# The first layer norm of an encoder layer, computed by tokens in place of features

## The chip, the cores and the metric

One core of a Trainium2 chip runs the whole kernel. The metric is the device time of one execution in microseconds (us), lower being better. The engines named below are TensorE (PE, with its weight loads PEld), VectorE (DVE), ScalarE (ACT), GpSimd (POOL) and SyncE (SP, which issues transfers).

## The reference

One encoder layer: 16 meta tokens are put ahead of 512 tokens of width 1024, and four layer norms stand around a feed-forward block, a token mixer and a second feed-forward block. The change touches the first norm, whose result `h` feeds the first feed-forward block and the residual.

```python
def layer_norm(x, g, b):
    xf = x.astype(jnp.float32)
    mu = jnp.mean(xf, axis=-1, keepdims=True)
    xc = xf - mu
    var = jnp.mean(xc * xc, axis=-1, keepdims=True)
    return (xc * lax.rsqrt(var + LN_EPS) * g + b).astype(x.dtype)

def swiglu(h, w_gate, w_up, w_down):
    return (jax.nn.silu(h @ w_gate) * (h @ w_up)) @ w_down
...
    h = layer_norm(jnp.concatenate([meta, x], axis=1), ln_in_g, ln_in_b)
    for i in range(DEPTH):
        h = layer_norm(DN_ALPHA * h + 0.5 * swiglu(h, ffn1_w_gate[i], ffn1_w_up[i], ffn1_w_down[i]),
                       ffn1_ln_g[i], ffn1_ln_b[i])
```

## The kernel before, in words

Activations lie with features on the partitions: `X` and `H` are 128 x 8 x 528 float32 (eight tile columns `k` of 128 features, 528 tokens), and `xs` holds the norm's scaled output as two float16 parts, high (`xs[:, 0]`) and low (`xs[:, 1]`). Matmuls of float32 quality are made of three float16 products (high x high, low x high, high x low). So each weight chunk, too, is split. A chunk is the gate and up weights of one tile of 128 hidden features, 128 x 2048 float32 in one of two slots of `stage`. VectorE takes its absolute maximum (`chunk_max`), GpSimd the maximum over partitions, VectorE makes a power-of-two scale of it (`chunk_scale`), ScalarE writes the high part to `wsp` (`split_hi`) and VectorE the low part (`chunk_lo`, which signals `w_ready`). SyncE loads the next chunk into a slot once its low part is written.

The order on each engine is written out by hand, and engines meet at semaphores. The first norm (L = 0) ran like the others, in two halves of 264 tokens: VectorE sums the eight tiles (`x_sum`, L1770), TensorE multiplies by a matrix of 1/1024 to spread the mean over the partitions (L465), VectorE subtracts it (`centre`, L1257), ScalarE squares (L918), TensorE adds the squares up over features (L470), ScalarE takes the root (L932), VectorE the reciprocal (L1277) and multiplies (L1281), and ScalarE writes the high part of `xs` (L943) and `H` (L945) with gain and bias as scale and bias columns. VectorE writes the low part (`split_lo`, L1271). `layer_norm_scales` (L1745 on) computes the powers of two for three norms from the parameters. Between these steps stand the maxima, scales and splits of chunks 0 and 1.

The first feed-forward block starts with `gu_tile` for tile 0 (`first=True`): for each tile column `k` it waits for the high part (`x_hi`) and the low part (`x_ready`), 12 matmuls of 264 columns each. Tiles 1 to 21 need the whole of `xs` and their own chunk, 96 matmuls each. ScalarE applies Silu to a tile's gate half (L958), VectorE multiplies by the up half (`hidden_tile`, L1342). Then VectorE turns to the chunk two tiles on.

## Time and profile before

| what | value |
|---|---|
| median of 3 runs | 1099.26 us (1098.03 to 1104.86) |
| the profiled execution's own time | 1098.44 us |
| its span | 1096.6 us |
| TensorE busy | 1005.5 us (92%) |
| VectorE busy | 730.0 us (67%) |
| ScalarE busy | 385.6 us (35%) |
| mean granted clock of TensorE | 0.972 of 2.4 GHz |

The span is the time from the first to the last instruction of one profiled execution, and its own time contains it. A busy TensorE is not TensorE at its peak, since matmuls are pipelined. The shares are means over stages with different limits: what an edit at the start is worth is read from the start.

### The profile page before, as it was taken

The page shows a single profiled execution, that of the slowest core. Times are in us where ns is not written, and L with a number is a line of the kernel's source. Part 1 is how long each engine was busy: PE and PEld are TensorE (multiplying, and loading weights), DVE is VectorE, ACT ScalarE, POOL GpSimd, SP SyncE. Part 2 cuts the span into 40 slices and gives each one's busy share as a digit, 9 for nine tenths or more (in the row PEclk, how much of TensorE's full clock was granted, in tenths as well). Part 3 has the DMA queues.
Part 4 walks back from the last instruction along what each step waited for, and adds up shares of the span by engine and source line. Part 5 has one row for each costly group of instructions (what it writes and reads, how often), then busy time and mean ns, then how long its engine had stood idle before and what let it go on. Part 6 is the DMA issues. An engine that isn't in the chain of part 4 may idle for free.

```text
span 1096.6 us, 16402 instructions
## 1 busy us (share of the span) xinstructions
PE 1005.5 (92%) x6604; PEld 658.2 (60%) x6604; DVE 730.0 (67%) x1188; ACT 385.6 (35%) x492; POOL 33.8 (3%) x96
## 2 busy tenths in 40 slices
PE   2799999999899997999996889779999999989995
PEld 1588888888688874895565434434444444434443
DVE  7756666668865657777658857676666666876645
ACT  2722222224511117655234742362222222541105
POOL 1000000000000000000000000000000000000000
PEclk9899999999899998999998989889999999999998
DMA  4232232323313220221211002213232232312202
GB/s 157 71 114 101 90 111 80 115 77 140 109 54 106 96 77 1 78 78 40 76 40 39 1 1 77 77 39 113 79 115 103 88 115 90 145 56 103 105 1 78
DMA packets 25168, 88.70 MB, mean 81 GB/s; under 512 B 2859, under 2 KB 5123, under 8 KB 25123
## 3 DMA queue, kind: packets, MB, share of 16 engines
q1 hardware_dynamic: 24256, 87.24, 22.7%
q10 hardware_dynamic: 867, 0.85, 0.3%
q8 instruction: 29, 0.48, 0.2%
q14 instruction: 16, 0.13, 0.0%
HBM read 85.99 MB, written 2.10 MB: 80 GB/s over the span
## 4 chain that ended last, share of the span: by engine, by line
PE 75%; DVE 15%; ACT 7%; issue 2%; DMA 1%; ACTq 0%; POOL 0%; DVEq 0%
PE PS L485 35%; PE PS L521 20%; PE PS L576 8%; PE PS L872 3%; DVE cmax L1308 3%; DVE wsp L1330 3%; PE PS L470 2%; ACT wsp L951 2%; ACT H L945 2%; DVE X L1257 1%; PE PS L560 1%; PE PS L850 1%; DVE big L1408 1%; ACT xs L943 1%; PE PS L698 1%
## 5 line engine op out<-in xcount | busy, mean ns | idle before, releaser
L485 PE MATMUL PS<-xs,wsp 128*128 128x264 f16 (+1 forms) x3168 | 471.6, 312 | 12.8 <-ACT xs L943 8.1
L485 PEld LDWEIGHTS PS<-xs,wsp 128*128 128x128 f16 x3168 | 310.6, 98 | 173.8 <-issue 13.5
L951 ACT ACTIVATE wsp<-stage,wscale 128x2048 f16<-128x2048 f32 (+2 forms) x73 | 156.5, 2144 | 370.5 <-DVE wscale L1294 198.6
L1330 DVE SCALAR_TENSOR_TENSOR wsp<-stage,wscale,wsp 128x2048 f16<-128x2048 f32 (+2 forms) x73 | 184.6, 2529 | 113.9 <-ACT wsp L951 113.9
L521 PE MATMUL PS<-big,wsp 128*128 128x264 f16 (+1 forms) x1584 | 238.5, 314 | 11.6 <-DVE big L1408 9.5
L521 PEld LDWEIGHTS PS<-big,wsp 128*128 128x128 f16 x1584 | 155.8, 99 | 94.0 <-DVE big L1408 12.8
L1308 DVE TENSOR_REDUCE cmax<-stage 128x1 f32<-128x2048 f32 (+2 forms) x73 | 179.7, 2461 | 3.9
L1342 DVE SCALAR_TENSOR_TENSOR big<-PS,oscale,tmp_a 128x528 f32 (+3 forms) x44 | 33.4, 758 | 75.8 <-ACT tmp_a L958 75.8
L958 ACT ACTIVATE tmp_a<-PS,oscale 128x528 f32<-128x528 f32 (+1 forms) x44 | 30.5, 693 | 135.9 <-PE PS L485 135.9
L576 PE MATMUL PS<-xs,wsp 128*128 128x264 f16 (+1 forms) x384 | 67.0, 328 | 0.1
L1842 POOL PARTITION_ALL_REDUCE call<-cmax x73 | 29.5, 404 | 984.2 <-DVE cmax L1308 984.2
L470 PE MATMUL PS<-tmp_b,ones 128*128 128x264 f32 (+1 forms) x128 | 36.2, 445 | 17.5 <-ACT tmp_b L918 17.5
L576 PEld LDWEIGHTS PS<-xs,wsp 128*128 128x128 f16 x384 | 35.8, 98 | 24.4 <-issue 1.9
L872 PE MATMUL PS<-xs,wsp 128*128 128x512 f16 x192 | 42.4, 379 | 3.2 <-DVE X L1354 2.1
L470 PEld LDWEIGHTS PS<-tmp_b,ones 128*128 128x128 f32 x128 | 27.9, 223 | 26.1 <-ACT tmp_b L918 21.1
L918 ACT ACTIVATE tmp_b<-X 128x264 f32<-128x264 f32 (+1 forms) x64 | 23.9, 416 | 49.5 <-DVE X L1257 45.7
L576 PE MATMUL PS<-wsp,xs 128*88 128x256 f16 (+2 forms) x408 | 39.5, 257 | 1.7 <-ACT kT L1013 1.7
L981 ACT ACTIVATE big<-big,hscale 128x528 f16<-128x528 f32 (+1 forms) x44 | 30.3, 722 | 29.1 <-DVE big L1408 26.5
L576 PEld LDWEIGHTS PS<-wsp,xs 128*88 128x88 f16 (+2 forms) x408 | 38.0, 113 | 3.5 <-ACT kT L1013 2.5
L1408 DVE SCALAR_TENSOR_TENSOR big<-big,hscale 128x528 f16<-128x528 f32 (+1 forms) x44 | 31.6, 755 | 5.0 <-ACT big L981 3.8
L872 PEld LDWEIGHTS PS<-xs,wsp 128*128 128x128 f16 x192 | 18.5, 98 | 26.8 <-DVE wsp L1330 2.6
L1366 DVE SCALAR_TENSOR_TENSOR X<-PS,oscale,H 128x528 f32<-128x528 f32 (+1 forms) x16 | 12.2, 760 | 27.5 <-PE PS L521 27.4
(178 smaller groups left out, 694.4 us busy)
## 6 DMA issues: line engine op xcount, KB each, us to landing
stage<-in_gate SPq DMA_DIRECT2D x44, 512.0 KB, 3.7
stage<-in_up SPq DMA_DIRECT2D x44, 512.0 KB, 4.5
stage<-in_down SPq DMA_DIRECT2D x32, 704.0 KB, 4.9
stage<-in_w_in SPq DMA_DIRECT2D x16, 512.0 KB, 4.6
stage<-in_w_out SPq DMA_DIRECT2D x8, 512.0 KB, 4.3
X<-in_xT SPq DMA_DIRECT2D x2, 1056.0 KB, 6.9
out_T<-H SPq DMA_DIRECT2D x8, 256.0 KB, 2.0
stage<-in_w_in SPq DMA_DIRECT2D x2, 576.0 KB, 4.3
```

The lines of the kernel that those rows point to most:

```text
L470: nc.tensor.matmul(PS[:, ln_bank(L, 1, h), 0:ln_width(L)], ones[:, :], squares[:, n % 4, 0:ln_width(L)], start=k == 0, stop=k == KD - 1).t ...
L485: return nc.tensor.matmul(dst, w, x, start=k == 0 and wp + xp == 0, stop=k == KD - 1 and xp == 1)
L521: mm = nc.tensor.matmul(dst, w(wp, k), x, start=k in (0, split_at) and wp + xp == 0, stop=k + 1 in (kt, split_at) and xp == 1)
L576: mm = nc.tensor.matmul(dst, x if lhs_is_x else w, w if lhs_is_x else x, start=k == 0 and wp + xp == 0, stop=k == KD - 1 and xp == 1)
L872: mm = nc.tensor.matmul(acc(1, 2 * (n % 2)), w, tokens(1, xs[:, xp, k, :]), start=gla and k == REP and wp + xp == 0, stop=not gla and k == ...
L951: nc.scalar.activation(wsp[:, slot, 0, 0:cols], stage[:, slot, 0:cols], ACT.Copy, scale=wscale[:, slot:slot + 1]).then_inc(w_hi, 1)
L958: nc.scalar.activation(tokens(f, tmp_a[:, s, :]), acc(f, 4 * s), ACT.Silu, scale=oscale[:, slot:slot + 1]).then_inc(silu_ready, 1)
L981: nc.scalar.activation(hid_s[:, m, 0, ln_cols(2 * f)], hid[:, m + 2, ln_cols(2 * f)], ACT.Copy, scale=hscale[:, i:i + 1]).then_inc(hs_hi, 1)
L1308: nc.vector.tensor_reduce(cmax[:, one], stage[:, slot, 0:cols], AX.X, ALU.max, apply_absolute_value=True).then_inc(w_max, 1)
L1330: nc.vector.scalar_tensor_tensor(wsp[:, slot, 1, 0:cols], stage[:, slot, 0:cols], wscale[:, one], wsp[:, slot, 0, 0:cols], ALU.mult, ALU.s ...
L1342: nc.vector.scalar_tensor_tensor(tokens(f, hid[:, m + 2, :]), acc(f, 4 * s + 2), oscale[:, slot:slot + 1], tokens(f, tmp_a[:, s, :]), ALU. ...
L1408: nc.vector.scalar_tensor_tensor(hid_s[:, m, 1, t], hid[:, m + 2, t], hscale[:, i:i + 1], hid_s[:, m, 0, t], ALU.mult, ALU.subtract).then_ ...
```

## The change

The input comes with tokens on the partitions: four tiles `x_tok` of 128 tokens x 1024 features, in the memory of `X`, loaded by four transfers with chunk 0 after the second and chunk 1 last. Mean and variance are now one number per partition, held in `tok_stat`: a sum along the free axis on VectorE (on ScalarE for tile 2), a square with an accumulated sum on ScalarE with minus the mean as bias, a root and a reciprocal of one column, and one `tensor_scalar` that adds minus the mean and multiplies (`tok_norm`). TensorE transposes each 128 x 128 block into PSUM banks 4 to 7 (`turn`): tile columns 0 to 3 of all token tiles ahead of the first products, 4 to 7 inside tile 0 (`turn_late`). Gain and bias are applied where PSUM is read: ScalarE writes all high parts and the even tile columns of `H`, VectorE the odd ones (`tok_affine`) and the low parts (`tok_lo`). The 16 meta tokens come as a 128 x 128 tile, 8 partitions to a token, with a 128 x 128 matrix that averages over each 8; they have a path of their own beside the token tiles. The other norms are as they were; their counts of semaphores start at L = 1. The identity, until now loaded behind the first norm, is loaded at the start. The diff without the meta tokens' path, the semaphores' declarations and renumberings:

```diff
-        x_loaded = [sem(f"x_loaded{i}") for i in range(2)]
+        x_tok = X[:, :, :].rearrange("p k t -> p (k t)")[:, 0:N_TOK * D_MODEL].rearrange("p (i d) -> p i d", i=N_TOK)
+        meta_x, meta_ones = tmp_a[:, 0, 0:P], tmp_a[:, 0, P:2 * P]
+        tok_scratch = big[:, 0:(N_TOK + 2) * D_MODEL].rearrange("p (i d) -> p i d", d=D_MODEL)
...
-            for h in range(2):
-                sp.dma_start(X[:, :, token_half(0, h)], xT[h].rearrange("p (k t) -> p k t", k=KD)).then_inc(x_loaded[h], 16)
+            for i in range(N_TOK):
+                sp.dma_start(x_tok[:, i, :], x_in[i]).then_inc(x_loaded[i], 16)
+                if i == 1:
+                    load_gu(0, 0, 0)
+            load_gu(0, 1, 1)
...
-                    if L:
-                        pe.wait_ge(*((res_half, L) if h == 0 else (res_done, 2 + KD * L)))
-                        last = X[:, KD - 1, token_half(L, h)]
-                    else:
-                        pe.wait_ge(x_summed, h + 1)
-                        last = x_sum[:, token_half(L, h)]
-                    nc.tensor.matmul(PS[:, ln_bank(L, 0, h), 0:ln_width(L)], ones[:, :], last, start=L == 0, stop=True).then_inc(mean_ready, 1)
...
+            def turn(k, i):
+
+                return nc.tensor.transpose(PS[:, 4 + k % 4, P * i:P * (i + 1)], x_tok[:, i, P * k:P * (k + 1)], ident[:, :])
...
+                pe.wait_ge(ident_loaded, 16)
+                for i in range(N_TOK):
+                    pe.wait_ge(tok_normed, i + 1)
+                    for k in range(4):
+                        mm = turn(k, i)
+                        if i == N_TOK - 1:
+                            mm.then_inc(tok_turned, 1)
+                    if i == 1:
+                        pe.wait_ge(meta_normed, 1)
+                        nc.tensor.transpose(PS[:, 3, 0:P], meta_x, ident[:, :]).then_inc(meta_turned, 1)
+
+            def turn_late(k):
+
+                pe.wait_ge(x_ready, k - 3)
+                for i in range(N_TOK):
+                    mm = turn(k, i)
+                mm.then_inc(tok_turned, 1)
...
+                    if f == 0:
+                        pe.wait_ge(meta_lo, 1)
                     for k, g in itertools.product(range(KD), range(2)):
+                        if f == 0 and g == 1 and k >= 1 and k + 3 < KD:
+                            turn_late(k + 3)
...
-            layer_norm(0)
+            start_tokens()
...
+            act.dma_start(tmp_a[:, 0, 0:2 * P], meta_in).then_inc(meta_loaded, 16)
+            act.dma_start(ident[:, :], ident_in).then_inc(ident_loaded, 16)
...
+            def tok_square(i):
+                act.wait_ge(tok_mean, i + 1)
+                nc.scalar.activation(tok_scratch[:, i, :], x_tok[:, i, :], ACT.Square, bias=tok(MEAN, i),
+                                     accum_out=tok(VAR, i)).then_inc(tok_sq, 1)
+
+            def tok_root(i):
+                act.wait_ge(tok_sq, i + 1)
+                nc.scalar.activation(tok(ROOT, i), tok(VAR, i), ACT.Sqrt, bias=eps[:, 0:1],
+                                     scale=1.0 / D_MODEL).then_inc(tok_std, 1)
...
+                tok_square(0)
+                tok_root(0)
...
+                tok_square(1)
+                tok_root(1)
+                act.wait_ge(x_loaded[2], 16)
+                nc.scalar.activation(tok_scratch[:, N_TOK + 1, :], x_tok[:, 2, :], ACT.Copy, accum_out=tok(SUM, 2)).then_inc(tok_sum_2, 1)
+                tok_square(2)
+                tok_root(2)
+                split_hi(0, 0, GU_COLS)
+                tok_square(3)
+                tok_root(3)
...
+                for k in range(KD):
+                    if k == 5:
+                        split_hi(GU[0] + 1, 1, GU_COLS)
+                    x = PS[:, 4 + k % 4, 0:SEQ]
+                    act.wait_ge(tok_turned, k + 1)
+                    nc.scalar.activation(xs[:, 0, k, N_META:T], x, ACT.Identity, scale=par_s[:, C_G[0] + k:C_G[0] + k + 1],
+                                         bias=par_s[:, C_B[0] + k:C_B[0] + k + 1]).then_inc(x_hi, 1)
+                    if k % 2 == 0:
+                        nc.scalar.activation(H[:, k, N_META:T], x, ACT.Identity, scale=par[:, C_G[0] + k:C_G[0] + k + 1],
+                                             bias=par[:, C_B[0] + k:C_B[0] + k + 1]).then_inc(h_in, 1)
+
...
+            def tok_total(i):
+                dve.wait_ge(x_loaded[i], 16)
+                nc.vector.tensor_reduce(tok(SUM, i), x_tok[:, i, :], AX.X, ALU.add).then_inc(tok_sum, 1)
...
+            def tok_minus_mean(i, signal, at):
+                dve.wait_ge(signal, at)
+                nc.vector.tensor_scalar(tok(MEAN, i), tok(SUM, i), -1.0 / D_MODEL, None, ALU.mult).then_inc(tok_mean, 1)
+
+            def tok_norm(i):
+                dve.wait_ge(tok_std, i + 1)
+                nc.vector.reciprocal(tok(ROOT, i), tok(ROOT, i)).then_inc(tok_rstd, 1)
+                dve.wait_ge(tok_rstd, i + 1)
+                nc.vector.tensor_scalar(x_tok[:, i, :], x_tok[:, i, :], tok(MEAN, i), tok(ROOT, i),
+                                        ALU.add, ALU.mult).then_inc(tok_normed, 1)
...
+            def tok_affine(k):
+                if k % 2:
+                    dve.wait_ge(x_hi, k + 1)
+                    nc.vector.tensor_scalar(H[:, k, N_META:T], PS[:, 4 + k % 4, 0:SEQ], par[:, C_G[0] + k:C_G[0] + k + 1],
+                                            par[:, C_B[0] + k:C_B[0] + k + 1], ALU.mult, ALU.add).then_inc(h_in_v, 1)
+
+            def tok_lo(k):
+                dve.wait_ge(x_hi, k + 1)
+                dve.wait_ge(h_in_v if k % 2 else h_in, k // 2 + 1)
+                nc.vector.scalar_tensor_tensor(xs[:, 1, k, N_META:T], H[:, k, N_META:T], xscale[:, 0:1], xs[:, 0, k, N_META:T],
+                                               ALU.mult, ALU.subtract).then_inc(x_ready, 1)
+
...
+            dve.wait_ge(meta_loaded, 16)
+            nc.vector.tensor_reduce(tok(SUM, META), meta_x, AX.X, ALU.add).then_inc(meta_sum, 1)
+            tok_total(0)
+            tok_minus_mean(0, tok_sum, 1)
+            dve.wait_ge(meta_avg, 1)
+            nc.vector.tensor_scalar(tok(MEAN, META), PS[:, 3, P:P + 1], -1.0, None, ALU.mult).then_inc(meta_mean, 1)
+            tok_total(1)
+            tok_minus_mean(1, tok_sum, 2)
+            tok_norm(0)
+            meta_norm()
+            tok_norm(1)
             chunk_max(0, 0, 0, GU_COLS)
-            centre(0, 1)
+            tok_minus_mean(2, tok_sum_2, 1)
+            tok_total(3)
+            tok_minus_mean(3, tok_sum, 3)
             chunk_scale(0, 0, XF_GU[0])
...
+            meta_affine()
+            tok_norm(2)
             chunk_lo(0, 0, GU_COLS)
-            layer_norm(0, (1, 1, XF_GU[0]))
+            tok_norm(3)
+            dve.wait_ge(meta_hi, 1)
+            nc.vector.scalar_tensor_tensor(xs[:, 1, :, 0:N_META], H[:, :, 0:N_META], xscale[:, 0:1], xs[:, 0, :, 0:N_META],
+                                           ALU.mult, ALU.subtract).then_inc(meta_lo, 1)
+            for k in range(KD):
+                tok_affine(k)
+                tok_lo(k)
+                if k == 1:
+                    chunk_max(1, 1, 0, GU_COLS)
+                if k == 3:
+                    chunk_scale(1, 1, XF_GU[0])
...
-    tokens = np.concatenate([meta_tokens, x[0]], 0)
-    arrays = {"xT": kcols(tokens.T).reshape(P, KD, 2, HALF).transpose(2, 0, 1, 3).reshape(2, P, -1)}
+    segment = np.arange(P) // KD
+    block_mean = (segment[:, None] == segment[None, :]).astype(np.float32) / D_MODEL
+    arrays = {"x": x[0].reshape(N_TOK, P, D_MODEL), "meta": np.concatenate([meta_tokens.reshape(P, P), block_mean], 1)}
```

How the instructions stand now on two engines. In the rows a name is an instruction's output and inputs, and the bracket what it waits for.

The first place is VectorE in the norm. Before, from centring the first half on (`stats` is where sums and reciprocals lie, `cmax` a chunk's maximum, `call` the same over partitions):

```order
L1257 TENSOR_TENSOR X<-X,PS 128x264 [waits mean_ready,b_step]
L1257 TENSOR_TENSOR X<-X,PS 128x264 x7
L1308 TENSOR_REDUCE cmax<-stage 128x1 [waits w_loaded0]
...
L1308 TENSOR_REDUCE cmax<-stage 128x1 [waits w_loaded1]
L1330 SCALAR_TENSOR_TENSOR wsp<-stage,wscale,wsp 128x2048 [waits w_hi]
...
L1277 RECIPROCAL stats<-stats 128x264 [waits std_ready] x2
L1281 TENSOR_TENSOR X<-X,stats 128x528 [waits centred,rstd_ready]
L1281 TENSOR_TENSOR X<-X,stats 128x528 [waits centred] x2
L1271 SCALAR_TENSOR_TENSOR xs<-H,xscale,xs 128x528 [waits h_ready]
```

Behind the two halves' centring stand chunk 1's maximum, chunk 0's low part, the long reciprocals and the multiplications. After, from the second token tile's normalising to the fourth's:

```order
L1883 RECIPROCAL tok_stat<-tok_stat 128x1 [waits tok_std]
L1885 TENSOR_SCALAR X<-X,tok_stat 128x1024 [waits tok_rstd]
L1413 TENSOR_REDUCE cmax<-stage 128x1 [waits w_loaded0]
L1879 TENSOR_SCALAR tok_stat<-tok_stat 128x1 [waits tok_sum_2]
L1875 TENSOR_REDUCE tok_stat<-X 128x1 [waits x_loaded3]
L1879 TENSOR_SCALAR tok_stat<-tok_stat 128x1 [waits tok_sum]
...
L1885 TENSOR_SCALAR X<-X,tok_stat 128x1024 [waits tok_rstd]
L1435 SCALAR_TENSOR_TENSOR wsp<-stage,wscale,wsp 128x2048 [waits w_hi]
L1883 RECIPROCAL tok_stat<-tok_stat 128x1 [waits tok_std]
L1885 TENSOR_SCALAR X<-X,tok_stat 128x1024 [waits tok_rstd]
```

The centring passes over `PS` and the long reciprocals are gone, and chunk 1's maximum is no longer ahead of chunk 0's low part.

The second place is VectorE behind the first eviction, after (before, nothing but multiplications and low parts stood there):

```order
L1912 SCALAR_TENSOR_TENSOR xs<-H,xscale,xs 128x512 [waits h_in,x_hi]
L1906 TENSOR_SCALAR H<-PS,par 128x512 [waits x_hi]
L1912 SCALAR_TENSOR_TENSOR xs<-H,xscale,xs 128x512 [waits h_in_v,x_hi]
L1413 TENSOR_REDUCE cmax<-stage 128x1 [waits w_loaded1]
L1912 SCALAR_TENSOR_TENSOR xs<-H,xscale,xs 128x512 [waits h_in,x_hi]
L1906 TENSOR_SCALAR H<-PS,par 128x512 [waits x_hi]
L1912 SCALAR_TENSOR_TENSOR xs<-H,xscale,xs 128x512 [waits h_in_v,x_hi]
L1395 TENSOR_SCALAR cexp<-call 128x1 [waits w_all]
```

Chunk 1's maximum is now behind the low part of tile column 1 and ahead of that of column 2; the scale made from it follows after column 3.

The third place is ScalarE around chunk 1's split, where `xs` and `H` are written. Before, from tile column 3:

```order
L943 ACTIVATE xs<-X,par_s 128x528 [waits normed]
L945 ACTIVATE H<-X,par 128x528
L951 ACTIVATE wsp<-stage,wscale 128x2048 [waits w_scale]
L943 ACTIVATE xs<-X,par_s 128x528 [waits normed]
L945 ACTIVATE H<-X,par 128x528
```

The split stood ahead of tile column 4, two rows to a column. After, from `H` of column 2:

```order
L1033 ACTIVATE H<-PS,par 128x512
L1030 ACTIVATE xs<-PS,par_s 128x512 [waits tok_turned] x2
L1033 ACTIVATE H<-PS,par 128x512
L1059 ACTIVATE wsp<-stage,wscale 128x2048 [waits w_scale]
L1030 ACTIVATE xs<-PS,par_s 128x512 [waits tok_turned] x2
L1033 ACTIVATE H<-PS,par 128x512
```

It now stands ahead of column 5. Of eight rows on `H` four have gone to VectorE, and the source is `PS` in place of `X`.

On TensorE the column sums of ones are gone. Sixteen transposes, and one for the meta tokens, stand ahead of the products, and sixteen more inside tile 0 in groups of four, between the gate and the up products of tile columns 1 to 4, the group for column k waiting for the low part of column k - 4, whose bank it takes.

## Rows read from the trace of the kernel before

**Rows 1.** Chain of waits, first 75 us: start us, length us, what.

```profile
0.73 5.71 DMA X<-in_xT
...
6.46 7.30 DVE stats L1770 x2
...
15.87 2.81 DVE X L1257 x8
18.68 2.20 DVE cmax L1308
...
28.22 5.53 PE PS L470 x16
...
34.29 1.81 DVE stats L1277
...
38.41 0.72 ACT xs L943
...
42.72 1.89 ACT wsp L951
...
51.17 2.27 DVE wsp L1330
...
53.49 21.55 PE PS L485 x190
```

**Rows 2.** Windows: us; busy us (count) of PE, PEld, DVE, ACT, POOL; PEclk, DMA share, GB/s.

```profile
5.00:10.00 5.00, 0.00 (x0) 0.00 (x0) 3.54 (x1) 0.00 (x0) 0.00 (x0) 1.00 1.09 382
...
100.00:200.00 100.00, 100.00 (x892) 86.97 (x890) 61.59 (x88) 25.11 (x19) 3.50 (x10) 1.00 0.27 95
```

**Rows 3.** DMA issues of inputs: KB each, median us from issue to landing.

```profile
X<-in_xT SPq DMA_DIRECT2D x2, 1056.0 KB, 6.9
...
par<-in_params ACTq DMA_DIRECT2D x1, 38.5 KB, 1.9
```

**Rows 4.** VectorE in order of time, first of the scales: start us, us, what.

```profile
13.68 0.19 DVE L1747 TENSOR_REDUCE bmax<-par 128x6 f32<-128x48 f32 x1
```

**Rows 5.** VectorE groups by form: count, busy us, mean ns, idle before.

```profile
L1271 DVE SCALAR_TENSOR_TENSOR xs<-H,xscale,xs 128x512 f16<-128x512 f32 x8 | 6.0, 751 | 3.9 <-ACT H L945 3.7
...
L1292 DVE TENSOR_SCALAR cneg<-cexp 128x1 int32<-128x1 int32 x73 | 11.2, 154 | 2.5
...
L1298 DVE TENSOR_REDUCE hmax<-big 128x1 f32<-128x528 f32 x6 | 4.2, 693 | 0.0
...
L1478 DVE TENSOR_SCALAR tmp_b<-PS,par 128x528 f32<-128x528 f32 x4 | 3.1, 768 | 11.7 <-ACT tmp_a L1043 11.5
...
L1512 DVE TENSOR_SCALAR tmp_a<-tmp_a 128x528 f32<-128x528 f32 x4 | 1.7, 434 | 0.1
```

**Rows 6.** ScalarE groups by form.

```profile
L1177 ACT ACTIVATION_READ_ACCUMULATOR tmp_b<-tmp_b,smin 128x1 f32 x16 | 3.0, 186 | 0.0
...
L1200 ACT ACTIVATE xs<-PS,hscale 128x512 f16<-128x512 f32 x4 | 2.7, 676 | 4.6 <-PE PS L850 4.6
...
L1050 ACT ACTIVATE tmp_a<-tmp_a 128x1056 f32<-128x1056 f32 x2 | 2.2, 1084 | 0.0
...
L1013 ACT ACTIVATE kT<-PS,oscale 128x16 f32<-128x16 f32 x1 | 0.3, 263 | 0.0
```

**Rows 7.** TensorE, transposes by ident in the attention.

```profile
L832 PE MATMUL PS<-ident,tmp_b 128*128 128x128 f32 x56 | 9.0, 306 | 1.8 <-DVE tmp_b L1732 1.6
```

**Rows 8.** TensorE in order of time in tile 0, and windows of 1 us there.

```profile
39.27 7.07 PE L485 MATMUL PS<-xs,wsp 128*128 128x264 f16 x48 [0.82 <-DVE xs L1271]
...
41.00:42.00 1.00, 1.00 (x6) 0.72 (x5) 0.95 (x2) 1.00 (x3) 0.00 (x0) 0.50 0.00 0
...
43.00:44.00 1.00, 1.00 (x11) 0.87 (x10) 1.00 (x2) 1.00 (x1) 0.00 (x0) 1.00 0.00 0
```

**Rows 9.** VectorE in order of time, tile 0's hidden product and chunk 2.

```profile
53.34 0.76 DVE L1342 SCALAR_TENSOR_TENSOR big<-PS,oscale,tmp_a 128x528 f32<-128x528 f32 x1
...
59.55 2.35 DVE L1330 SCALAR_TENSOR_TENSOR wsp<-stage,wscale,wsp 128x2048 f16<-128x2048 f32 x1 [1.81 <-ACT wsp L951]
```

115 lines of the change are left out of this document (82 added, 33 removed).

## Prediction

> **What bounds the kernel now.** I read the chain of waits first, from the start of the span. Up to 53.49 us it runs through the first layer norm; from there TensorE's gate and up products follow one another [rows 1]. Its pieces are the first half of the input (5.71), the sums over the eight tiles (7.30), centring (2.81 twice), the first weight chunk's maximum (2.20), the squares' column sums (5.53), the reciprocal (1.81), a weight split on ScalarE (1.89) and the low half of chunk 1 on VectorE (2.27). Tile 1 of the gate and up products starts when that last one ends. The reader should take 53.49 as the number that decides. Behind it TensorE is busy for all of 100 us with 892 matmuls, one per 0.112 us, while VectorE is busy for 62 [rows 2]. A tile is 96 matmuls, 10.8 us. So what tile 1 gains in start, the end gains, as long as chunk 2 is ready in time and later stages, whose instructions are the same, don't care. The profiled execution's span is 1096.6 and its own time 1098.44; the median of the runs shown is 1099.26, 0.8 above. A change can be told from none here by about 1%, 11 us.
>
> **Inputs.** The input is now four token tiles of 512 KB with chunk 0 behind the second and chunk 1 last, and the meta tile (128 KB) and the identity (64 KB) come forward on ScalarE's queue. Before, 1056 KB were in at 6.44 [rows 1], and DMA moves 382 GB/s from 5 to 10 us [rows 2]. By bytes in queue order I place tile 0 at 5.4, tile 1 at 6.8, chunk 0 at 9.5, tiles 2 and 3 at 10.8 and 12.2, chunk 1 at 14.8. The estimate takes transfers in the order of issue; the half input's median of 6.9 us to landing [rows 3] says up to 1.5 later. The parameters land 1.9 us after an issue at 0.73 [rows 3], so the scales, which ran from 13.68 [rows 4] until centring began at 15.87 [rows 1], behind the sums, now run from 2.7 to 5.0 while VectorE would wait anyway: 2.2 us off the path.
>
> **Prices.** On VectorE a sum or maximum costs 693 ns for 528 columns and follows its predecessor 2.20 apart for 2048 [rows 1, 5], so a token sum of 1024 is 1.14. Normalising a tile (one tensor_scalar on 1024 columns, SBUF to SBUF, two column scalars) isn't in the trace. The nearest row, 128x528 in SBUF, is 434 ns against 154 for a one-column operation [rows 5]: 0.154 + 0.280 x 1024/528 = 0.70. If it went like the row that reads PSUM (768 ns), it would be 0.154 + 0.614 x 1024/528 = 1.35. I take 0.70, since source and target are the same kind as in the nearest row. H and low-half steps on 512 columns are 0.70 each (751 and 768 ns, less the overlap of neighbours), small ones 0.15. On ScalarE a pass over 1056 columns is 1084 ns, so 1.05 for 1024, plus 186 for reading the accumulator: 1.22 in a row of others. A root is 0.25 (263 for 16 columns), an eviction from PSUM 0.64 (676, less overlap) [rows 6]. A transpose is 9.0/56 = 0.16 on TensorE [rows 7], twice that at the low clock.
>
> **First stretch, to the last transposed token tile.** VectorE sets the pace, ScalarE twice holds it.
> - Sum 0 ends 6.6, its and the meta mean 7.0, sum 1 8.1. ScalarE squares meta and tile 0 to 8.7, roots to 9.2, square and root 1 to 10.7; VectorE waits for it and has tile 1 normalised at 11.7.
> - Maximum of chunk 0, 2.2: 13.9. Mean 2, sum 3, mean 3: 15.4 (tile 2's sum is on ScalarE, done at 12.1). Scale of chunk 0, five small ones: 16.1. Meta gain and bias: 16.8. Reciprocal and tile 2: 17.7.
> - ScalarE's split starts at 16.1 with the scale and ends at 18.0; the low half of chunk 0 ends at 20.3. Tile 3: 21.2, four transposes, the first at 21.5.
> What is removed by this from the chain: 7.30 of sums, about 5.6 of centring (2.81 for a half), 5.53 of sums of squares on TensorE and the reciprocal of 1.81 [rows 1]. Added instead are three sums, six ScalarE passes of 1.22 or less and four normalisings of 0.9.
>
> **Second stretch, the evictions.** The two multiplications of before (by rstd on VectorE, then xs and H on ScalarE, 0.72 each [rows 1]) become xs on ScalarE and H divided between both.
> - xs 0 and H 0 to 23.0, low half 0 to 23.8, H 1 and low half 1 to 25.3. The maximum of chunk 1 has moved in here, 2.2: 27.5. Low 2, H 3, low 3: 29.6. Scale of chunk 1: 30.3. Low 4: 31.0.
> - Behind that maximum wait TensorE's products for tile column 2 and, through them, the late transposes. Behind the scale waits ScalarE's split (30.3 to 32.2), which stands ahead of xs 5: VectorE idles from 31.0 to 32.9.
> - H 5, low 5, low 6, H 7, low 7, five times 0.7: 36.5. Low half of chunk 1, 2.27: 38.8. **Tile 1 starts at 38.9.**
> TensorE has 96 products and 16 late transposes in here. At the low clock a product is near 0.2 (6 starts or fewer in a microsecond), at the high one 0.11 [rows 8]. From 23.9 they run without long gaps; with four transposes at 0.32 and the rest of the time at 0.2 a product, 18 products (a column and a half) are done by 28, where I let the clock rise. What is left, 6.5 x 12 x 0.11 and 12 x 0.16, ends at 38.5, hidden under VectorE by 0.4 us. That cover is thin. Each microsecond more at the low clock costs 0.45: a clock up at 32 makes it 4 x 0.45 - 0.4 = 1.4 later (40.3), one at 36 3.2 later (42.1).
>
> **Behind it.** Chunk 2 becomes ready 8.5 us after VectorE begins tile 0's hidden product (53.34 to 61.9 [rows 9]). That now begins at 39.1, once ScalarE has issued its five constant DMAs and loaded its table: ready at 47.6, wanted at 38.9 + 10.8 = 49.7. The five DMAs now overlap chunk 3's load, which isn't wanted before 50. The sum: 53.49 - 38.9 = 14.6 us off; 1098.44 - 14.6 = 1083.8 for an execution like the profiled one, 1084.7 for the median.
>
> **Rival 1: prices at their upper ends.** Normalising at 1.35 adds 0.65 for each of the tiles 1, 2 and 3; the part of tile 2 runs while VectorE would wait for the split, so about 1.3. Transfers 1.5 later add up to 1.6. Together tile 1 starts near 41.5 and the time is 1087.3. For it: chunk 0's landing was never waited for before. Against: 528 columns in 434 ns.
>
> **Rival 2: the first tile stays at 1.2 GHz.** Granted clock was 0.50 at 41 to 42 us and 1.00 at 43 to 44, after TensorE had been at work since 39.27 [rows 8]. Now its work ahead of the tile is 17 transposes in short bursts. If it rises only after the tile: 96 x 0.2 + 16 x 0.32 = 24.3 from 21.8, and 1.3 for the first low half, gives 47.4: 6.1 us gained, 1093.2. Against: from 23.9 on the products are as dense as those that raised it before. The Trainium skill speaks against this change here: TensorE: Matmul & The Clock Gate, Part 4, says that transposes don't count as activity for the clock. By that rule the bursts would warm nothing, and the tile would begin at the low clock; the sum above already begins so, and the rule alone would not carry it to 47.4. No row here shows transposes alone.
>
> **Rival 3: slower.** The same clock stays low beyond the tile, through tiles 1 and 2. Each costs 96 x 0.112 = 10.8 more: 1093.2 + 21.6 = 1114.8. It decides from (6.1 + 11)/0.112, about 150 low-clock matmuls after tile 0, where 6.1 gained becomes 11 lost. Against: within 4 us of steady products the clock was up [rows 8], and nothing in tile 1 pauses.
>
> **Rival 4: more than forecast.** Chunk 1's split could find its place between two evictions without VectorE waiting (1.9 less), and ScalarE's passes of 1024 could cost 0.9 in place of 1.22 where VectorE waits for two of them (0.6 less): tile 1 at 36.4, 1082.2. Against the first: the order of ScalarE's queue is fixed, and xs 5 stands behind the split.
>
> **How the numbers follow.** Forecast 0.66, rival 1 0.15, rival 2 0.10, rival 3 0.02, rival 4 0.07. The forecast's own range is 1082 to 1087.5. The range given holds rivals 1 and 4 and the near part of rival 2 (a clock up at 36 or later): 1080.5 to 1090. Faster by over 1% is below 1088.3: the forecast, rival 4 and most of rival 1, 0.83. Rival 2 and the rest of rival 1 are within 1%: 0.15. Slower 0.02. The later stages' own clock dips fall elsewhere once all is shifted; I allow 1 us for them in the range.
>
> **What would show it.** VectorE's parameter scales end near 5.0; the tensor_scalar on 1024 columns takes 0.6 to 0.8; tile 3 is normalised near 21; the maximum of chunk 1 stands between low halves 1 and 2; VectorE idles for ScalarE near 31 to 33; the last low half before tile 1 ends near 38.8, and from tile 1 on every instruction has its old distance. It is wrong if TensorE, and not VectorE, ends last before tile 1, if token tiles are waited for beyond 8 us, or if TensorE waits for chunk 2.

## The result, and the profile of the changed kernel

The changed kernel takes 1083.12 us, the median of 4 runs (1082.67 to 1086.39), against 1098.64 us for the kernel before in the same comparison (4 runs, 1096.19 to 1104.86). The ratio is 0.986, 95% interval 0.9832 to 0.9888. The forecast was 1084.7. The profiled execution took 1082.67 us and its span is 1080.9, 15.7 less than before's 1096.6.

That the number came out near the forecast says little about its steps, so the profile is read against each. The first stretch, on VectorE (start us, length us, engine, line, output from input, shapes, and in brackets the idle time just before, with what ended it):

```profile
4.66 0.20 DVE L1852 TENSOR_REDUCE bmax<-par 128x6 f32<-128x48 f32 x1 [4.66 <-DMA par<-in_params]
...
18.07 0.81 DVE L1885 TENSOR_SCALAR X<-X,tok_stat 128x1024 f32<-128x1024 f32 x1
...
21.70 0.81 DVE L1885 TENSOR_SCALAR X<-X,tok_stat 128x1024 f32<-128x1024 f32 x1
...
24.64 0.75 DVE L1912 SCALAR_TENSOR_TENSOR xs<-H,xscale,xs 128x512 f16<-128x512 f32 x1 [1.86 <-ACT H L1033]
```

The parameters are waited for until 4.66. The two tensor_scalar rows normalise token tiles 2 and 3; the last row is the first low half of the transposed input. In the chain of waits (start us, length us, what) the same stretch reads:

```profile
0.73 3.91 DMA par<-in_params
...
7.15 1.14 DVE tok_stat L1875
...
10.66 1.14 ACT big L996 x2
...
13.16 2.19 DVE cmax L1413
...
26.89 2.28 DVE cmax L1413
...
31.87 2.00 ACT wsp L1059
...
38.48 2.27 DVE wsp L1435
```

None of before's long pieces is left ahead of the evictions: 7.30 of sums, the two passes of centring of 2.8 each, the 5.53 of column sums on TensorE and the 1.81 of reciprocal [rows 1]. A token sum of 1.14, a ScalarE pass of 1.14, and the maxima of the two chunks are what the chain holds instead. The first eviction, ScalarE's first write of `xs` from the 512 tokens, in the kernel before (of the 528) and then here:

```profile
36.87 0.83 ACT L943 ACTIVATE xs<-X,par_s 128x528 f16<-128x528 f32 x1 [2.61 <-DVE X L1281]
```

```profile
23.09 0.78 ACT L1030 ACTIVATE xs<-PS,par_s 128x512 f16<-128x512 f32 x1 [2.13 <-PE PS L515]
```

It starts 13.8 us earlier. TensorE, from its last token tile to the second tile of products (the same columns as VectorE's rows):

```profile
24.01 1.04 PE L553 MATMUL PS<-xs,wsp 128*128 128x264 f16 x4 [0.32 <-ACT xs L1030]
25.45 3.26 PE L553 MATMUL PS<-xs,wsp 128*128 128x264 f16 x14 [0.40 <-DVE xs L1912]
28.50 1.06 PE L515 MATMUL PS<-ident,X 128*128 128x128 f32 x4
29.36 1.81 PE L553 MATMUL PS<-xs,wsp 128*128 128x264 f16 x12
31.00 0.60 PE L515 MATMUL PS<-ident,X 128*128 128x128 f32 x4
...
35.01 5.07 PE L553 MATMUL PS<-xs,wsp 128*128 128x264 f16 x42
40.80 31.45 PE L553 MATMUL PS<-xs,wsp 128*128 128x264 f16 x278 [0.73 <-DVE wsp L1435]
```

Tile 1 starts at 40.80, where before had 53.49 [rows 1]: 12.7 us earlier, not the 14.6 of the forecast. So all of the gain is made ahead of the first eviction; from it to tile 1 the changed kernel takes 17.7 us and the one before 16.6, a loss of 1.1. From 25.45 to 40.08 TensorE has no gap, then it waits 0.73 us for VectorE. So there are two chains of nearly the same length here, which the experiments take apart.

From there the two kernels keep their distance. VectorE's low half of a weight chunk that stands at 114.85 us in the trace of the kernel before stands here:

```profile
102.17 2.35 DVE L1435 SCALAR_TENSOR_TENSOR wsp<-stage,wscale,wsp 128x2048 f16<-128x2048 f32 x1 [1.81 <-ACT wsp L1059]
```

114.85 - 102.17 = 12.68. This low half is the **mark** of all comparisons below: it is far enough behind the start that everything in the first tiles has settled, and ahead of anything else that differs. But the spans differ by 15.7, so 3.0 us came from somewhere later. By VectorE's instructions, which are the same there, the distance is 12.5 until 627 us of the changed kernel and 15.6 from 632 on, inside the attention. The windows there (us; busy us and count of PE; the clock granted; DMA share; GB/s) of the changed kernel:

```profile
620.00:624.00 4.00, 2.52 (x18) 0.98 0.00 0
624.00:628.00 4.00, 4.00 (x18) 0.59 0.00 0
628.00:632.00 4.00, 3.13 (x18) 1.00 0.00 0
```

and of the kernel before, some 13 us later:

```profile
636.00:640.00 4.00, 4.00 (x14) 0.54 0.00 0
640.00:644.00 4.00, 4.00 (x16) 0.50 0.00 0
644.00:648.00 4.00, 4.00 (x19) 0.68 0.02 4
648.00:652.00 4.00, 2.94 (x13) 1.00 0.00 0
```

The granted clock is at its lower level (0.50, 1.2 GHz) for 3.4 us in the one and 10.2 us in the other, in a stage whose instructions are the same in both. The change's design has no part in that, or so it looks; the first experiment asks.

### The profile page after: what moved, and what is told of

The parts are those of the page before. It is cut to its first block, busy times and chain, and to the rows that moved or that the text cites. A ratio compares the mean times of both kernels' runs of the same rounds, so it can differ in the third digit from the quotient of the medians.

```text
span 1080.9 us, 16392 instructions
## 1 busy us (share of the span) xinstructions
PE 997.0 (92%) x6605; PEld 654.4 (61%) x6605; DVE 720.4 (67%) x1186; ACT 382.2 (35%) x488; POOL 32.3 (3%) x96
## 4 chain that ended last, share of the span: by engine, by line
PE 75%; DVE 16%; ACT 6%; issue 2%; DMA 0%; ACTq 0%; POOL 0%; DVEq 0%
PE PS L553 35%; PE PS L593 20%; PE PS L648 8%; DVE cmax L1413 3%; DVE wsp L1435 3%; PE PS L944 3%; ACT wsp L1059 2%; PE PS L510 2%; PE PS L632 1%; DVE big L1513 1%; ACT H L1053 1%; PE PS L770 1%; DVE X L1363 1%; PE PS L922 1%; PE PS L766 1%
## 5 line engine op out<-in xcount | busy, mean ns | idle before, releaser
L648 PE MATMUL PS<-wsp,xs 128*88 128x256 f16 (+2 forms) x408 | 39.5, 257 | 1.7 <-ACT kT L1121 1.7
L992 ACT ACTIVATE tmp_b<-X 128x256 f32<-128x256 f32 (+1 forms) x48 | 17.8, 416 | 46.6 <-DVE X L1363 45.3
L510 PE MATMUL PS<-tmp_b,ones 128*128 128x256 f32 (+1 forms) x96 | 24.9, 417 | 9.9 <-ACT tmp_b L992 9.9
L1403 DVE TENSOR_REDUCE hmax<-big (+2 forms) x44 | 30.1, 684 | 0.0
```

The source lines that it names most:

```text
L510: nc.tensor.matmul(PS[:, ln_bank(L, 1, h), 0:ln_width(L)], ones[:, :], squares[:, n % 4, 0:ln_width(L)], start=k == 0, stop=k == KD - 1).t ...
L648: mm = nc.tensor.matmul(dst, x if lhs_is_x else w, w if lhs_is_x else x, start=k == 0 and wp + xp == 0, stop=k == KD - 1 and xp == 1)
```

## The experiments

The theory after the result: the start is worth 12.7 us, VectorE's chain sets it, and TensorE's work in tile 0 stands 0.7 us behind it; the other 3.0 us are the attention's clock and belong to no edit. The rivals: that the attention's gain is the change's own; that the move of chunk 1's maximum, or the scales ahead of the sums, and not the cheaper norm, gives much of the gain; and that TensorE with its slow clock at the start is the real bound.

One table holds the measured times. The mark is VectorE's low half of above; the gain is counted from 114.85, the kernel before. "Tile 1" is where its products start; where TensorE runs without a gap into tile 1, it is the start of the last 42 products of tile 0 plus the 5.07 us of the changed kernel's row; in scales_first_max_moved, where it runs so too, the end of chunk 1's low half.

```
kernel                   tile 1   mark     gain    median us (runs)   interval of the ratio
before                   53.49    114.85    -      1097.42 to 1100.31
changed                  40.80    102.17   12.68   1083.12 (4)        0.9832 to 0.9888
again                    40.81    102.17   12.68   1089.30 (6)        0.9863 to 0.9934
max_early                40.68    102.05   12.80   1085.85 (4)        0.9844 to 0.9914
max_idle                 40.2     101.54   13.31   1084.14 (4)        0.9832 to 0.9904
warm_pe                  40.70    102.07   12.78   1088.50 (6)        0.9862 to 0.9938
idle_and_warm            39.8     101.10   13.75   1087.48 (4)        0.9850 to 0.9934
idle_warm_params         40.0     101.27   13.58   1085.43 (6)        0.9859 to 0.9925
double_max               43.39    104.76   10.09   1093.38 (1)
two_products             40.90    102.26   12.59   1091.60 (1)
idle_two_products        38.02     99.38   15.47   1088.96 (1)
scales_first             51.29    112.66    2.19   1095.60 (10)       0.9967 to 1.0008
scales_first_max_moved   55.8     117.23   -2.38   1098.88 (10)       0.9992 to 1.0025
```

The runs come from four sets, each with executions of the kernel before beside it, against which the ratio is taken: its median was 1098.64 for the first row, 1098.50 for again, max_early, max_idle and warm_pe, 1097.42 for the next two and the two scales_first, and 1100.31 for the three of a single execution. The mark resolves 0.1 us: in two executions of the changed kernel it stands at the same 0.01, but chunk 0's low half, ahead of which most of the edited kernels are alike, starts between 19.20 and 19.34. The medians don't follow the mark, as max_idle against idle_and_warm shows. The reason is the first experiment's subject.

**again: the changed kernel, unedited.**

> The changed kernel once more, unedited. Theory A (the norm's chain is worth 12.7 us, and the 3.0 us more that the two profiles differ by is chance in the attention, where TensorE's clock was low for 3.4 us in one trace and 10.2 in the other): tile 1 of the gate and up products starts at 40.8 +- 0.1 again, while the time moves by up to 3 us between executions of the same kernel, with the whole of it in stretches behind the first tile. Theory B (the change brings the attention's 3.0 us too): the attention is as short in this trace as in the last one, and the times stay 15 to 16 us below those of before in every execution.

Its six runs lie from 1082.68 to 1092.17. In the profiled one (1091.32, span 1089.5) the mark stands at 102.17, the same to 0.01 us as in the first trace, and tile 1 starts at 40.81. All of the 8.6 us between the spans arise later. The attention's windows of this execution:

```profile
608.00:612.00 4.00, 3.32 (x16) 0.55 0.00 0
612.00:616.00 4.00, 4.00 (x10) 0.50 0.02 4
616.00:620.00 4.00, 4.00 (x22) 0.67 0.00 0
...
632.00:636.00 4.00, 4.00 (x18) 0.50 0.00 0
636.00:640.00 4.00, 4.00 (x15) 0.61 0.00 0
```

Two stretches of 10.2 us at the lower clock (from 608.4 and from 628.9), where the first execution had one of 3.4. One and the same program thus gains on the kernel before 12.68 at the mark and 15.7 at the end in one execution, 12.68 and 7.1 in another. The 3.0 us are an execution's, not the change's. Of the 8.6 us between the two executions 7.8 arise in the attention and 1.1 in the stages from 280 to 450 us; 0.2 come back behind them. All thirteen traces bear this out. The clock is low in this part of the attention (600 to 660 us) for 10.2 us in the kernel before. Where it is low for 3.4 (changed, max_idle, idle_warm_params, scales_first_max_moved), the distance to the kernel before grows there by 3.0; where for 10.2 (max_early, warm_pe, scales_first), it stays within 0.1; where for 20.5 (the other five), it shrinks by 4.6 to 4.8. No edit goes with these three cases, and the changed kernel itself is in two of them. The 3.0 us of the first execution were also the reason why the number seemed right: 12.7 that the start gives, and 3.0 that this execution gave on top, make the 15.8 between 1098.44 and 1082.67.

**max_early: chunk 1's maximum back ahead of chunk 0's low half, its scale ahead of the evictions.**

```diff
+            chunk_max(1, 1, 0, GU_COLS)
...
+            chunk_scale(1, 1, XF_GU[0])
...
             for k in range(KD):
                 tok_affine(k)
                 tok_lo(k)
-                if k == 1:
-                    chunk_max(1, 1, 0, GU_COLS)
-                if k == 3:
-                    chunk_scale(1, 1, XF_GU[0])
```

> One part of the change undone: the maximum of chunk 1 stands ahead of chunk 0's low part again, and its scale ahead of the evictions. Theory V (VectorE alone sets tile 1's start): the first low half comes 1.8 us later (2.2 less 0.4 of idle time), but 2.2 + 0.7 go from among the evictions and ScalarE's split no longer holds VectorE for 1.8: chunk 1's low half ends 3.2 us earlier, tile 1 starts at 37.6, the time falls by 3. Theory T (TensorE, at its low clock up to 29.95 us, is the next bound, 0.7 us below): its products start 1.8 us later, tile 0 ends at 41.9 in place of 40.08, tile 1 starts at 42.0, 1.2 us later than in the changed kernel.

Neither theory's number came: the mark moves by 0.12 us, tile 1 starts at 40.68. The other order gains nothing here: VectorE's 2.28 us are spent earlier, and it then waits for ScalarE instead, whose split of chunk 1 still stands behind evictions that need late transposes. The waits of VectorE from 16 to 41 us (waited for, us in total, times, longest):

```profile
DVE xs L1912 <- ACT H L1033: 2.1, 2, 1.2
DVE H L1906 <- ACT xs L1030: 1.7, 1, 1.7
```

TensorE is close behind in this run too: it waits 0.22 us at tile 1, so not more than 0.34 could have been gained, whatever the order is worth to VectorE.

**max_idle: the same maximum where VectorE would idle 1.86 us for ScalarE's first eviction, its scale two columns earlier, and ScalarE's split of chunk 1 one column earlier (the last hunk).**

```diff
+            chunk_max(1, 1, 0, GU_COLS)
             for k in range(KD):
                 tok_affine(k)
                 tok_lo(k)
-                if k == 1:
-                    chunk_max(1, 1, 0, GU_COLS)
-                if k == 3:
+                if k == 1:
                     chunk_scale(1, 1, XF_GU[0])
...
-                    if k == 5:
+                    if k == 4:
```

> Chunk 1's maximum moved into VectorE's 1.86 us of idle time ahead of the first low half, its scale behind tile column 1, ScalarE's split ahead of column 4. Theory V: the first low half 0.4 later, everything behind it 2.2 earlier and the idle 1.8 at column 5 gone or less: tile 1 at 38 to 38.9, 2 to 3 us gained. Theory T: TensorE's products are continuous from 25.45 to 40.08 in the changed kernel and now start 0.4 later: tile 0 ends at 40.4, tile 1 at 40.5, 0.3 us gained.

With 1.86 us of idle time filled, the mark moves by only 0.63. TensorE now runs without a gap into tile 1 (x325 is one row from tile 0 far into the next ones), and VectorE waits 2.9 us in four places for evictions of which most wait for transposes:

```profile
25.65 3.26 PE L553 MATMUL PS<-xs,wsp 128*128 128x264 f16 x14 [0.64 <-DVE xs L1912]
...
35.18 37.01 PE L553 MATMUL PS<-xs,wsp 128*128 128x264 f16 x325
```

Chunk 1's low half is ready at 40.1, TensorE begins tile 1 at 40.2. So the bound has passed to TensorE, 0.6 us below where VectorE's chain had it. (Counted by matmul records, of which some are missing, this kernel's gain reads as 0.1; two expectations below rest on that. The mark counts nothing.)

**warm_pe: 15 more matmuls of ones by ones between the first transposes.**

```diff
                     if i == 1:
                         pe.wait_ge(meta_normed, 1)
                         nc.tensor.transpose(PS[:, 3, 0:P], meta_x, ident[:, :]).then_inc(meta_turned, 1)
+                    for _ in range((0, 10, 5, 0)[i]):
+                        nc.tensor.matmul(PS[:, 0, 0:P], ones[:, :], ones[:, :], start=True, stop=True)
```

> Fifteen matmuls of a constant matrix, into a PSUM bank that tile 0 overwrites, fill TensorE's idle time between the transposes of the token tiles (14.5 to 18.9 and 20.1 to 22.6 us). If the clock goes by TensorE's own recent work, it rises before the first product: products 0.11 us apart from the start, late transposes a third as long, TensorE waits for VectorE in between. Theories V and T both: VectorE's chain ends at 40.7 as before, and the time stays within 0.3 us at tile 1. A rival, that products at the low clock hold back the late transposes and so ScalarE and VectorE: then tile 1 comes up to 1.5 us earlier.

The clock does rise sooner, at 15.7: four transposes take 0.66 instead of 1.12, and the first 14 products 1.98 instead of 3.26. The mark moves by 0.10. TensorE spends what it won on waiting for VectorE:

```profile
22.62 0.66 PE L515 MATMUL PS<-ident,X 128*128 128x128 f32 x4 [1.86 <-DVE X L1887]
...
25.34 1.98 PE L555 MATMUL PS<-xs,wsp 128*128 128x264 f16 x14 [0.83 <-DVE xs L1914]
...
36.20 3.77 PE L555 MATMUL PS<-xs,wsp 128*128 128x264 f16 x32 [0.89 <-DVE xs L1914]
40.70 1.52 PE L555 MATMUL PS<-xs,wsp 128*128 128x264 f16 x12 [0.73 <-DVE wsp L1437]
```

So in the changed kernel as it stands the slow clock at the start costs nothing. Each chain hides the gain of the other. That calls for both edits at once.

**idle_and_warm: both.**

> Both edits of max_idle and warm_pe together: chunk 1's maximum taken on VectorE before chunk 0's low half, and 15 extra matmuls of ones by ones (their output is overwritten) on TensorE between the transposes of the first norm, so that its granted clock is up by about 16 us. Alone, max_idle left tile 1 starting only 0.1 us earlier (VectorE then waits 2.9 us in all for evictions that wait for transposes at the low clock), and warm_pe alone left it where it was (VectorE's chain of 40.7 us as before). If the two limits stand level, each hides the other's gain, and here transposes of 0.66 us for four leave no such waits: VectorE's low halves end at 37.5, tile 1 starts at 37.5 to 38.3, 2.5 to 3.3 us earlier than in the changed kernel, offset to the kernel before 15.2 to 16.0. If a third thing holds it (ScalarE's split and evictions, 0.67 to 0.78 us each), tile 1 stays at 40 or later. Time in the first case 1080 to 1083 us, in the second 1083 to 1086.

Neither number came: the mark moves by 1.07, more than by either edit (0.63 and 0.10), and by less than the 2.5 to 3.3 expected. TensorE again has no gap:

```profile
25.69 2.61 PE L555 MATMUL PS<-xs,wsp 128*128 128x264 f16 x14 [1.22 <-DVE xs L1914]
...
30.73 0.60 PE L515 MATMUL PS<-ident,X 128*128 128x128 f32 x4
31.17 1.51 PE L555 MATMUL PS<-xs,wsp 128*128 128x264 f16 x12
32.52 0.60 PE L515 MATMUL PS<-ident,X 128*128 128x128 f32 x4
```

These rows give the floor that I had not worked out. Row starts at the high clock: four transposes 0.44, twelve products 1.35, so 0.11 each. From 25.69, when the first low half is there, 92 products and 16 transposes are left: 92 x 0.1125 + 16 x 0.11 = 12.1, which ends at 37.8 at best. In this execution the clock was down again from 26.4 to 29.8; half speed for 3.4 us costs 1.7: 39.5, and tile 1 starts at 39.8. The same sum for the changed kernel: from 25.45, with the clock low until 29.95, 12.1 + 2.25 = 14.35 ends at 39.8, where the trace has 40.08. So this run did not relieve TensorE of the low clock, and its 1.07 is less than two relieved chains would give.

**idle_warm_params: also the parameters first on SyncE's queue, and token tile 0's sum ahead of the meta row's.**

```diff
+            sp.dma_start(par[:, :], params).then_inc(par_loaded, 16)
             for i in range(N_TOK):
                 sp.dma_start(x_tok[:, i, :], x_in[i]).then_inc(x_loaded[i], 16)
...
-            act.dma_start(par[:, :], params).then_inc(par_loaded, 16)
...
+            tok_total(0)
...
-            tok_total(0)
```

> As idle_and_warm, and the scale and bias parameters are loaded as the first transfer of SyncE's queue instead of ScalarE's, with the sum of the meta row behind that of token tile 0 on VectorE. In the changed kernel the parameters landed at 3.9 us and VectorE stood 4.66 us for them; here they land by 2.3 to 2.6, the scales end at about 5.2 instead of 6.83, and if VectorE's chain is what sets the start of tile 1, that moves forward by another 1.4 to 1.7 us, to 35.9 to 36.8. If the token tiles' landing sets the first sum instead (5.4 us at the earliest), the gain is 0.5 us or less. Time 1078.5 to 1081.5 in the first case.

The parameters are there at 2.83 us instead of 4.66, but token tile 0 is now what the sums wait for, and behind that the meta row's mean:

```profile
2.83 0.20 DVE L1854 TENSOR_REDUCE bmax<-par 128x6 f32<-128x48 f32 x1 [2.83 <-DMA par<-in_params]
...
5.87 1.22 DVE L1877 TENSOR_REDUCE tok_stat<-X 128x1 f32<-128x1024 f32 x1 [0.87 <-DMA X<-in_x]
...
8.02 0.16 DVE L1923 TENSOR_SCALAR tok_stat<-PS 128x1 f32<-128x1 f32 x1 [0.68 <-PE PS L521]
```

Of the 1.83 us, 0.35 are left when tile 3 is normalised (21.35 against 21.70), and none at the mark (0.17 later than idle_and_warm). The clock was low from 23.0 to 29.8 here, so 4.5 us of the products ran at it instead of 3.4, which costs about 0.55 and eats the 0.35. The same edit makes VectorE wait 0.68 for the meta row's mean, so 0.35 may be too little for what the late parameters cost.

**two_products and idle_two_products: TensorE relieved.** Both kernels leave out a third of tile 0's products, 3.6 us of TensorE's work by 0.1125 each (the expectation's 4.0 is too much). If two chains are level, taking work from one must show nothing in the changed kernel and the full gain in max_idle.

```diff
                         for wp, xp in PRODUCTS:
+                            if f == 0 and wp == 1:
+                                continue
```

> The changed kernel without one of the three products of tile 0 of the first feed-forward (32 of 96 matmuls left out, those of the weights' low part). It takes 4.0 us of work at the high clock from TensorE, and leaves VectorE and ScalarE their work. If VectorE's chain sets the start of tile 1, it stays at 40.2 to 40.8 (only the waits for evictions that stand behind late transposes, up to 1.8 us, can shrink). If TensorE's work does, tile 1 moves forward by 1.5 us or more, to 39.3 or less.

> max_idle without the same third of tile 0's products. In max_idle tile 1 started at about 40.7 with TensorE never idle from 25.65 on, and VectorE waited 2.9 us in four places for evictions that stood behind TensorE's transposes. If TensorE is the bound there, both gains now show: VectorE's waits fall under 1 us, chunk 1's low half is complete at 37.6 to 38.6 instead of 40.1, and tile 1 starts then, 2.0 to 3.0 us earlier than in max_idle. If ScalarE's own evictions and split were the cause of VectorE's waits, they stay above 2 us and tile 1 starts at 40 or later.

In the changed kernel tile 1 starts at 40.90, unmoved (in this execution chunk 0's low half, ahead of the edit, is 0.10 late already), with the wait for VectorE grown from 0.73 to 1.41. In max_idle it starts at 38.02, and the mark moves by 2.16:

```profile
35.75 0.85 PE L553 MATMUL PS<-xs,wsp 128*128 128x264 f16 x6 [0.17 <-DVE xs L1914]
38.02 12.21 PE L553 MATMUL PS<-xs,wsp 128*128 128x264 f16 x107 [1.41 <-DVE wsp L1437]
```

VectorE's waits for ScalarE's evictions fall from 2.9 to 1.0 us. This settles it: the three moves of max_idle are worth 2.88 us to VectorE's chain (102.26 - 99.38, both with two products), and with the whole of tile 0's products TensorE lets 0.63 of them through. These are single executions, read at the mark.

**double_max: VectorE's chain made longer.**

```diff
                 if k == 1:
                     chunk_max(1, 1, 0, GU_COLS)
+                    nc.vector.tensor_reduce(tok(SUM, 0), stage[:, 1, 0:GU_COLS], AX.X, ALU.max, apply_absolute_value=True)
```

> The changed kernel with chunk 1's maximum (2.28 us on VectorE) read a second time at the same place, its result unused. In the changed kernel VectorE idles 1.81 us behind column 4 for ScalarE's eviction, and TensorE waits 0.73 us at tile 1. If VectorE's chain sets the start of tile 1, it moves from 40.80 to 42.9 to 43.1; if the idle 1.81 us behind column 4 absorbs part, to 41.3 or less; if ScalarE's split of chunk 1, which waits for the scale behind the maximum, is what is late, also the later evictions move and tile 1 starts at 43 or more.

Tile 1 starts at 43.39, the third case: 2.59 later, for a row of 2.28 whose follower starts 2.19 later. VectorE's idle 1.81 us stays, since ScalarE's split is behind the scale and shifts with it:

```profile
36.73 0.81 DVE L1906 TENSOR_SCALAR H<-PS,par 128x512 f32<-128x512 f32 x1 [1.81 <-ACT xs L1030]
```

A cost on this chain counts in full. The other 0.4 are in one place of this single execution: the low halves behind this row start 1.35 after it, in the changed kernel 0.91; why is open. From the changed kernel one can lose at once and gain only 0.7 before TensorE is the bound.

**scales_first and scales_first_max_moved: parts of the change in the kernel before.** The scales ahead of the input's sums, instead of behind them:

```diff
+            layer_norm_scales()
...
-            layer_norm_scales()
```

> The kernel before, with one edit: the eight scales of the weights' first pieces are computed ahead of the sums of the first norm instead of behind them, so that they lie under the input's transfer. If the start is VectorE's chain, the 2.2 us of scales leave it and tile 1 starts at 51.2 to 51.5 instead of 53.49, 2.0 to 2.2 us of the 12.7 that the change gives; the rest (10.5 us) is then the cheaper statistics and evictions. If the order of the queues gave most of the change's gain, tile 1 would start below 47. Time 1096.0 to 1096.8.

The mark moves by 2.19 and tile 1 by 2.20 (51.29), as the prediction had priced it. The times agree in sign (1095.6 against 1097.42), but their interval holds 1. Then chunk 1's maximum and scale as well, into the loop of low halves as in the change:

```diff
+                    if L == 0 and k == 3:
+                        chunk_max(1, 1, 0, GU_COLS)
+                    if L == 0 and k == 5:
+                        chunk_scale(1, 1, XF_GU[0])
...
-            chunk_max(1, 1, 0, GU_COLS)
             chunk_lo(0, 0, GU_COLS)
-            layer_norm(0, (1, 1, XF_GU[0]))
+            layer_norm(0)
```

> scales_first, and chunk 1's maximum and scale moved on VectorE's queue to where the change puts them: among the low halves of chunk 0 (behind columns 3 and 5) instead of ahead of them. On a chain without idle time the order changes nothing but what ScalarE can begin: tile 1 at 51.0 to 51.8, as in scales_first within 0.4 us. If the moved maximum is itself a source of the gain it starts 2 us or more earlier (49.3 or less).

A miss on both expectations: the mark is 4.57 later than in scales_first. On the old norm the maximum ran under a wait, and out of it VectorE stands idle. Its second reciprocal, in this kernel and then in scales_first:

```profile
33.37 1.80 DVE L1277 RECIPROCAL stats<-stats 128x264 f32<-128x264 f32 x1 [5.32 <-ACT stats L932]
```

```profile
32.10 1.80 DVE L1277 RECIPROCAL stats<-stats 128x264 f32<-128x264 f32 x1 [2.81 <-ACT stats L932]
```

1.27 of the 4.57 is the column sums of squares, which took 6.71 us instead of 5.52 (the mean granted clock from 26 to 32 us was 0.50, in scales_first 0.72); whether the edit or the execution did that is open. 2.2 are the maximum itself, now on the chain. 0.7 are more waiting among the evictions (4.35 in all instead of 3.66), where ScalarE's split is late because the scale is. The last 0.4 is most of what the scale's five small steps take (0.70), which ran under the same wait as the maximum. So the new order alone is a loss, of 3.3 us even without the clock's share; the medians of ten runs each differ by 3.3. What is left for the rest of the change, the new norm with its loads and evictions, is 12.68 - 2.19 = 10.5 us. That is a subtraction: no run takes the statistics, the load by tokens or the transposes apart. The traces say only that it all lies ahead of the first eviction. It comes with an order of VectorE's work that leaves up to 2.88 us of its chain unused.

## Why the prediction came out as it did

- **What bounds it.** Right. Tile 1's start is what the end gains, as far as the start goes: the distance at the mark (12.68) is that of tile 1's start (12.69). That "later stages, whose instructions are the same, don't care" was wrong: their clock takes or gives up to 8.6 us between two executions of one program. I had allowed 1 us for it.
- **Inputs.** "The parameters land 1.9 us after an issue at 0.73" failed: 3.91 in the chain. The row is of a kernel where two transfers of 1056 KB ran beside it; now four of 512 KB do, and why that delays it was not tested. The scales therefore ended at 6.83, not 5.0, the first sum at 8.28, not 6.6. What came back at tile 3 without it is 0.35, in idle_warm_params. That the scales leave the path for 2.2 us is shown (2.19).
- **Prices.** The tensor_scalar of 1024 columns took 0.81, and its follower began 0.73 after it: the lower of the two bounds was right, and rival 1's 1.35 not. The token sum took 1.14 as forecast, the ScalarE pass 1.13 and the accumulator 0.19 (1.22 was given for both, spaced 1.26). Root 0.29 for 0.25. ScalarE's evictions from PSUM were taken at 0.64 and took 0.78, spaced 0.67. VectorE's `H` and low half took 0.81 and 0.75, forecast at 0.70 apart: behind a low half the next step starts 0.67 later, but behind `H` the low half of the same column, which reads it, 0.91 later (34.58 to 35.49), 0.2 more for each of the four odd columns. A transpose was taken at 0.16 and follows another at 0.11.
- **First stretch.** Everything stands 1.2 to 1.7 late: tile 1 normalised at 13.1 for 11.7, chunk 0's maximum done at 15.3 for 13.9, its low half at 21.6 for 20.3, tile 3 at 22.4 for 21.2. It was the start of the sums that carried through. The order and the two waits for ScalarE (0.70 for a root, 0.36 for the split) are as forecast.
- **Second stretch.** The idle time of VectorE for the split was given as 31.0 to 32.9 and was 32.8 to 34.6, 1.8 long for 1.9. The maximum stands between low halves 1 and 2. Tile 1 at 40.80 for 38.9: 1.2 of the 1.9 us from the first stretch, the rest in the first eviction (low half 0 done at 25.3 for 23.8) and the spacing of the others.
- **TensorE.** The clock was to be up by 28 and the tile to end at 38.5, covered by 0.4. It rose at 29.95 in this execution and at 28.1 in the next, the tile ended at 40.08, the cover was 0.73. (The record of the granted clock begins with that rise, and the windows ahead of it print 1.00; that the level was the lower one is read from the rows, 14 products in 3.26 us against 12 in 1.51.) Right in kind: VectorE ends last, and that is why a clock 2 us later or sooner made no difference (40.80 and 40.81). The Trainium skill's rule on transposes (TensorE: Matmul & The Clock Gate, Part 4), that they don't count as activity for the clock, did not decide. Ahead of the products TensorE had transposes in bursts of 1.1 us with gaps of up to 4.4, and the clock was low, as the rule says; short bursts of any matmul might have left it low too, and no run here separates the two.
- **Rival 2** (tile 0 all at 1.2 GHz) did not happen, nor did **rival 3**. **Rival 4** named a real gain, chunk 1's split without VectorE's wait, but overlooked that TensorE could not follow: its 36.4 lies 2.1 below the 38.5 at which the forecast itself has TensorE's work end. In the runs, idle_and_warm has tile 1 at 39.8, and even with the clock up throughout the work ends at 37.8.
- **Behind it.** Chunk 2's low half starts at 47.05 and ends at 49.4, for 47.6, and tile 2 wants it at 40.80 + 10.8 = 51.6: no wait, as forecast. The five constant DMAs and the table load delayed the hidden product by nothing (40.85).
- **The sum.** 14.6 was forecast for the start, 12.7 came; 0 for the rest, 3.0 came, by chance. Over the six runs of the second set, at a median of 1089.3, the kernel gains 9 us on its neighbour's 1098.5; the first set showed 15.5. Both are the same program. Over all ten executions of it the median is 1086.4, against 1098.5 over the seventeen of the kernel before beside them: 12.1 us, near the mark's 12.7, and three of the ten lie above the range's 1090. That the first set's median is 1.6 below the forecast, and not above it, is luck: the start came 1.9 short.

## What to carry to other kernels

When a change shortens the chain that sets a stage's start, work out at once what the second chain needs at its best (here 92 products and 16 transposes of 0.11 us, behind the first operand), since it is the floor of every further step; two chains within a microsecond hide each other's gains, and only a run that relieves both at once, or one after the other, shows them. Price a step at a mark behind it in the trace, not by the time of the whole kernel: here the mark repeated to 0.01 us in two executions whose times differ by 8.6. And a piece of work that ran under a wait costs its full length, and what hangs on it, once it is moved out.

## What the runs showed of the hardware that I had not expected

- The low-clock stretches of the attention differ between executions of one program: 3.4 us in all from 600 to 650 us in one, 20.5 in another, for spans of 1080.9 and 1089.5. What sets them off was not tried.
- Fifteen fp32 matmuls of 128 columns (30 rows in the trace) between the transposes brought the clock up at about 16 us in all three kernels that have them. In warm_pe the rise at 15.7 came 1.3 us behind the first of them (14.39), and transposes had run since 13.27; whether these had a part in it is open. There it stayed up. In idle_and_warm it fell again at 26.4, behind a gap of 1.22, in idle_warm_params already at 23.0. The gap ahead of both, 1.86 from 20.8 or 20.4 us on, stands in warm_pe too, so no gap explains the three; why it fell in two of them is open. The windows of idle_warm_params around the fall (us; busy us and count of PE; the clock granted; DMA share; GB/s):

```profile
22.00:23.00 1.00, 0.66 (x4) 1.00 0.56 135
23.00:24.00 1.00, 0.49 (x3) 0.51 1.02 397
```

- A load of 38.5 KB landed 3.9 us after its issue instead of 1.9, with the same queue and the same issue time of 0.73, when 512 KB transfers of other shape ran beside it and two more loads stood behind it on its queue; as the first transfer of SyncE's queue, ahead of them all, it took 2.1 (idle_warm_params). What of this delays it was not tried.
